# Projections of a 256-token transformer block on plain float32 weights instead of three float32r products

## The reference, cut to what matters

```python
for l in range(2):                                   # first block
    mod = silu(c) @ w_mod[l] + b_mod[l]              # 2048 -> 6144: shift, scale, gate
    h = rmsnorm(x, norm_gain[l]) * (1 + scale) + shift
    proj = h @ w_in[l]                               # 2048 -> 7504 columns
    ...                                              # sparse attention, retention, gates
    x = x + gate * (y @ w_out[l])                    # 2048 -> 2048
# second block, 16 meta tokens ahead of x
proj = rms_norm(h, norm_mix) @ w_in_2                # 2048 -> 7176
...                                                  # stick-breaking and forgetting attention
h = h + merged @ w_out_2                             # 2048 -> 2048
q = rms_norm(h, norm_ffn) @ peer_w_query             # 2048 -> 2048
...                                                  # top 16 of 16384 experts for 8 heads
a = gelu(einsum('thkd,td->thk', u[idx], h))          # 128 rows of 2048 floats for each token
out = h + einsum('thk,thkd->td', g * a, v[idx])
```

## Time and profile before

| | us |
|---|---|
| median of 3 runs | 3126.39 (3125.57 to 3129.42) |
| the profiled execution, its span | 3121.8 |
| TensorE busy | 2089.0 (67%) |
| VectorE busy | 1836.5 (59%) |
| ScalarE busy | 853.8 (27%) |
| GpSimd busy | 800.9 (26%) |
| moved by DMA | 900.9 MB, mean 289 GB/s |

### The profile page before, as it was taken

One profiled execution on the slowest core, in us unless ns is written; L12 is line 12 of the kernel. 1 busy time (PEld: TensorE's weight loads), 2 busy tenths in 40 slices (PEclk: granted clock), 3 DMA queues, 4 the chain that ended last, 5 costly groups with the idle time before them and its releaser, 6 DMA issues.

```text
span 3121.8 us, 29077 instructions
## 1 busy us (share of the span) xinstructions
PE 2089.0 (67%) x11378; PEld 1478.6 (47%) x11378; DVE 1836.5 (59%) x2711; ACT 853.8 (27%) x1267; POOL 800.9 (26%) x680
## 2 busy tenths in 40 slices
PE   5888989989999999999999983223232322322235
PEld 2676777888787787666668871000000000000001
DVE  3679886566776664343336697766565555564430
ACT  1334544444454454544545420000000000000000
POOL 1111110000000000000000036665555555555552
PEclk8999999999999999999999996566656566666667
DMA  9887875557665545334226699999999999999998
GB/s 385 289 293 263 296 259 150 184 182 248 210 189 153 164 158 172 111 122 132 85 82 201 194 377 403 422 422 421 421 422 421 422 421 419 421 421 421 421 421 346
DMA packets 244741, 900.90 MB, mean 289 GB/s; under 512 B 20759, under 2 KB 45613, under 8 KB 178413
## 3 DMA queue, kind: packets, MB, share of 16 engines
q0 software_dynamic: 94208, 612.85, 48.9%
q1 hardware_dynamic: 149152, 284.53, 27.8%
q10 hardware_dynamic: 1244, 1.67, 0.2%
HBM read 894.78 MB, written 2.10 MB: 287 GB/s over the span
## 4 chain that ended last, share of the span: by engine, by line
PE 45%; DMA 29%; DVE 10%; ACT 3%; issue 3%; POOL 2%; ACTq 0%; POOLq 0%; DVEq 0%
PE pp L1818 38%; DMA late<-in_peer_v,MI 9%; DMA P<-in_peer_v,MI 5%; PE tp L1818 5%; DMA x<-in_peer_v,MI 5%; DMA ring<-in_peer_v,MI 4%; DVE wL L1130 3%; DMA SY<-in_peer_v,MI 2%; PE tp L1821 2%; ACT wH L626 1%; DMA ring<-in_peer_w_query 1%; DVE UHM L1286 1%; DMA ring<-in_w_in 1%; POOL late L2361 1%; DVE P L1777 0%
## 5 line engine op out<-in xcount | busy, mean ns | idle before, releaser
L1130 DVE TENSOR_TENSOR wL<-ring,wH 128x1024 fp32r<-128x1024 f32 (+3 forms) x504 | 583.2, 1161 | 573.7 <-ACT wH L626 572.4
L1818 PE MATMUL pp<-wH,hH 128*128 128x512 f32 (+3 forms) x1888 | 745.7, 395 | 35.5 <-DVE wL L1130 19.4
L1818 PE MATMUL pp<-wL,hH 128*128 128x512 f32 (+3 forms) x1888 | 721.4, 382 | 0.0
L1818 PE MATMUL pp<-wH,hL 128*128 128x512 f32 (+3 forms) x1888 | 720.5, 382 | 0.0
L626 ACT ACTIVATE wH<-ring 128x1024 fp32r<-128x1024 f32 (+3 forms) x504 | 508.3, 1011 | 729.7 <-PE pp L1818 548.0
L1818 PE MATMUL pp<-late,S 128*32 128x512 f32 x768 | 232.6, 879 | 335.7 <-DMA x<-in_peer_v,MI 156.3
L1818 PEld LDWEIGHTS pp<-wH,hH 128*128 128x128 f32 x1888 | 362.3, 192 | 141.2 <-issue 46.3
L1818 PEld LDWEIGHTS pp<-wH,hL 128*128 128x128 f32 x1888 | 361.6, 192 | 64.1
L1818 PEld LDWEIGHTS pp<-wL,hH 128*128 128x128 f32 x1888 | 362.8, 192 | 57.3 <-issue 1.0
L1777 DVE CUSTOM_DVE_ANT_0 late<-late,P 128x2048 f32<-128x2048 f32 x84 | 191.2, 2288 | 155.2 <-DMA late<-in_peer_u,MI 155.2
L1818 PE MATMUL pp<-P,S 128*32 128x512 f32 x360 | 162.7, 898 | 166.9 <-DMA late<-in_peer_v,MI 93.2
(11 more groups left out here) (305 smaller groups left out, 2985.2 us busy)
## 6 DMA issues: line engine op xcount, KB each, us to landing
ring<-in_w_in SPq DMA_DIRECT2D x288, 512.0 KB, 4.4
ring<-in_w_out SPq DMA_DIRECT2D x96, 512.0 KB, 4.2
P<-in_w_mod POOLq DMA_DIRECT2D x85, 512.0 KB, 5.1
late<-in_w_mod SPq DMA_DIRECT2D x64, 512.0 KB, 9.4
SY<-in_w_mod POOLq DMA_DIRECT2D x43, 512.0 KB, 5.5
ring<-in_w_in SPq DMA_DIRECT2D x48, 368.0 KB, 4.8
ring<-in_peer_w_query SPq DMA_DIRECT2D x32, 512.0 KB, 7.9
ring<-in_w_in SPq DMA_DIRECT2D x24, 344.0 KB, 3.2
```

Of the source, the lines that this page charges most:

```text
L1130: tt(lo, raw, hi.bitcast(F32), ALU.subtract).then_inc(*tick("dve_lo", *names))
L1818: return e.matmul(o, l, r, start=start, stop=stop, skip_group_check=skip)
```

## The change

Weights and h are no longer cut. `three` becomes one product of plain float32 operands; `wH`, `wL`, `hH`, `hL` and `late` go, one `hT` stays. A piece waits for its load itself and frees the ring slot itself. The ring has 14 slots, and loads are issued 11 pieces ahead. The first 64 loads of w_mod pass through the last 8 ring slots; gathers have 14 buffers, five of them free at once as before, two in `hT` and seven in the ring from the end of p6 on. A chunk of h is written half by ScalarE and half by VectorE, and each half has its own mark. ScalarE has two new waits for its own earlier work ("squared", "attended").

```diff
-NB, NS, NG = 3, 4, 11
+NS, NG = 14, 14
+AHEAD = NS - 3
...
-    def splits(p, q):
-        while asked[0] < min(place[p, q] + NB, len(where)):
-            yield "split", *where[asked[0]]
+    def fetches(p, q):
+        while asked[0] < min(place[p, q] + AHEAD, len(where)):
+            yield "fetch", *where[asked[0]]
             asked[0] += 1
...
-    mod_in = [*[late[:, 1024 * b:1024 * b + 1024] for b in range(8)], P[:, 0, GA:GA + 1024], P[:, 1, GA:GA + 1024],
+    mod_in = [*[ring[:, NS - 8 + b, :] for b in range(8)], P[:, 0, GA:GA + 1024], P[:, 1, GA:GA + 1024],
...
                 if r >= NS:
                     w.wait_ge(*at("ring used", r - NS))
+                elif r >= NS - 8:
+                    w.wait_ge(*at("mod used", 56 + r - (NS - 8)))
...
-                act(heads(wH[k % NB][:, 0:2 * wd], 2), raw, ACT.Copy).then_inc(*tick("act_hi", ("hi", k)))
...
-                tt(lo, raw, hi.bitcast(F32), ALU.subtract).then_inc(*tick("dve_lo", *names))
...
+                    for j in (2, 3):
+                        k = 4 * c + j
+                        ts(hT[:, k, :], tp[u % 2][:, j * 256:j * 256 + 256], mcol[:, l, 16 + k:17 + k], mcol[:, l, k:k + 1],
+                           ALU.mult, ALU.add).then_inc(*tick("dve_h", *([("chunk turned", u), ("chunk", p, c, 1)] if j == 3 else [])))
...
-                w.wait_ge(*at("lo", k))
-                w.wait_ge(*at("chunk", p, pc // 2))
+                raw = heads(ring[:, r % NS, 0:2 * wd], 2)
+                w.wait_ge(*at("raw", r))
+                w.wait_ge(*at("chunk", p, pc // 2, pc % 2))
...
-                        hs = hH[:, kk, t * 128:(t + 1) * 128], hL[:, kk, t * 128:(t + 1) * 128]
-                        m = three(pp[b][:, 0:wd], hs, (hi[:, k2, :], lo[:, k2, :]), kk == 0, kk == 15)
+                        m = mm(pp[b][:, 0:wd], hT[:, kk, t * 128:(t + 1) * 128], raw[:, k2, :], kk == 0, kk == 15)
...
-                elif slot == 5:
-                    w.wait_ge(*at("lo", LAST_CUT))
-                elif slot == 7:
+                elif slot == 5:
                     w.wait_ge(*at("grouped", 6, 3))
```

More of the change, by code:

```diff
@@ L195, in project @@
         for q, (n, c0, w, pc) in enumerate(PIECES[p]):
-            yield from splits(p, q)
+            yield from fetches(p, q)
             if p in (0, 2) and n == 0:
@@ L324, in order @@
     for q, (g, c0, w, pc) in enumerate(PIECES[6]):
-        yield from splits(6, q)
+        yield from fetches(6, q)
         if q == 3:
@@ L404, in mixer_peer_program @@
         rsd = sb("rsd", [128, 6])
[L405 to L410, removed]
+        hT = sb("hT", [128, NK, 256])
         ident = CW[:, ID:ID + 128]
@@ L512, in slots, with parts @@
                 had[i] = n
-        def parts(p, c):
-            step = 2 if p in (1, 3) and c < 2 else 1
-            return [(k, step) for k in range(4 * c, 4 * c + 4, step)]
+        def parts(p, k0):
+            step = 2 if p in (1, 3) and k0 < 8 else 1
+            return [(k, step) for k in range(k0, k0 + 2, step)]
         def gain(p, k):
@@ L582, in sync @@
             for what, *a in order():
-                if what == "split":
+                if what == "fetch":
                     p, q = a
@@ L616, in store_rows @@
                                     xP[q:128:4, t, d * 512:(d + 1) * 512]).then_inc(*landed(sem, ("out", t, d, q)))
[L617 to L625, removed]
-                act(heads(wH[k % NB][:, 0:2 * wd], 2), raw, ACT.Copy).then_inc(*tick("act_hi", ("hi", k)))
+            turn, side = itertools.count(), itertools.count()
             def norm(p):
@@ L823, in sparse @@
                         w.wait_ge(*at("top", l, t, g))
+                        if (t, g) != (0, 0):
+                            w.wait_ge(*at("attended", l, *((t, 0) if g else (t - 1, 1))))
                         for h in range(4):
@@ L1764, in vector @@
                     for b0 in (0, 8):
-                        next(loads)
                         u = next(turn)
@@ L1826, in pair @@
                     w.wait_ge(*at("pair free", had_pair[u % 2]))
+                    if had_pair[u % 2] in by_two:
+                        w.wait_ge(*at("chunk turned", had_pair[u % 2]))
                 had_pair[u % 2] = u
                 return tp[u % 2], u
-            def three(o, l, r, first, final, skip=False):
-                mm(o, l[0], r[0], first, False, skip)
-                mm(o, l[0], r[1], False, False, skip)
-                return mm(o, l[1], r[0], False, final, skip)
             def chunk(p, c):
                 pr, u = pair()
+                by_two.add(u)
                 if p in (1, 3):
@@ L1865, in piece @@
                         kk = pc * 2 + k2
-                        hs = hH[:, kk, t * 128:(t + 1) * 128], hL[:, kk, t * 128:(t + 1) * 128]
-                        m = three(pp[b][:, 0:wd], hs, (hi[:, k2, :], lo[:, k2, :]), kk == 0, kk == 15)
-                    names = [("cut used", k)] if t else []
+                        m = mm(pp[b][:, 0:wd], hT[:, kk, t * 128:(t + 1) * 128], raw[:, k2, :], kk == 0, kk == 15)
+                    names = []
+                    if t and not (p == 4 and meta_part(c0, wd)):
+                        names.append(("ring used", r))
+                    elif t and pc % 2:
+                        names += [("ring used", raw_of[p, q - 1]), ("ring used", r)]
                     if pc == 7:
@@ L2263, in tensor @@
                     tr(pr[:, 512:608], stk2[0:96, :], 96).then_inc(*tick("pe_turned", ("turned", u)))
-                elif what == "split":
+                elif what == "fetch":
                     raw_of[a[0], a[1]] = next(loads)
-                    cut_of[a[0], a[1]] = next(ahead[0])
                 elif what == "chunk":
@@ L2282, in tensor @@
                     n, c0, wd, pc = PIECES[6][a[0]]
-                    k = next(cut)
-                    hi, lo = (heads(b[k % NB][:, 0:2 * wd], 2) for b in (wH, wL))
+                    r = raw_of[6, a[0]]
+                    raw = heads(ring[:, r % NS, 0:2 * wd], 2)
                     if pc == 0:
                         pr6, u6 = pair()
-                    w.wait_ge(*at("lo", k))
-                    w.wait_ge(*at("chunk", 6, pc // 2))
+                    w.wait_ge(*at("raw", r))
+                    w.wait_ge(*at("chunk", 6, pc // 2, pc % 2))
                     for b in range(4):
```

90 lines of the change are left out of this document (32 added, 58 removed).

## The result

| | before | after |
|---|---|---|
| median, 4 runs each (us) | 3126.06 | 3275.42 (3274.48 to 3277.49) |
| ratio, 95% interval | | 1.0481 (1.0462 to 1.0500) |
| span of the profiled execution (us) | 3121.8 | 3272.9 |
| TensorE busy (us) | 2089.0 | 2355.9 |
| VectorE, ScalarE busy (us) | 1836.5, 853.8 | 1253.7, 345.6 |

The change makes the kernel 4.8% slower; 14% faster was forecast. VectorE and ScalarE lost what they were expected to lose, and TensorE gained 267 us where it should have lost some 500.

The account below looks back on a forecast made before the run. PE was taken to bound the projections (DMA in p0 after the change) and DMA the gathers; the stage times summed to 2681 us of span, plus 4.6 gives 2686 us. 2630 to 2780 us held some 82%.

Parts of the forecast that it names:

- What a product costs: Projections p0 to p6: a plain float32 product of 512 columns takes 0.43 us, against 0.6915 for three float32r products.
- Rival (b): Projections: the array passes more often in long accumulating runs, 0.86 to 0.92 us per product, 3410 to 3500 us; chance 3%.
- Rival (a): Projections: a low granted clock makes a plain product 0.86 us or more, kernel ending near 3410 us; chance 3%.
- p0: First projection: bound by DMA at 343 GB/s, 364 us instead of 452.5.
- p1, p3, p5: These projections: TensorE still sets the time, 55, 58.5 and 60.2 us, with loads at 305 GB/s.
- rival (c): Weight loads in p0 to p3 and p5 get 250 GB/s, not 343: + 152, 2838 us; chance 5%.
- p2 and p4: These projections: 290 us (now 405.1) and 395 us (now 504.2), with 8 and 9 us added.
- Rival (d): Chains between pieces bound: PE's 44 us idle in p2 and p4 triples instead of growing by 17, 2756 us; chance 17%.
- p6 to the first gather: Start of p6 up to the first gather of expert rows: 31.5 us, with 9.0 less for products and 1.2 for a split.
- The gathers: First gather to the end: 1313.4 us instead of 1324.4, 11 us less because query weights have landed earlier.
- Start and gap: Start before p0 falls from 104.3 to 101.2 us, gap between p1 and p2 from 13.0 to 9.9.
- The splits: Dropping 504 rounding copies (ScalarE) and 504 subtractions (VectorE): these lie nearly nowhere on PE's path.

Follow-up runs that it names:

- e2: Kernel after, each projection product replaced by two equal bf16 products of the upper halves of the same bytes: 2640.59 us, ratio 0.8441.
- e3: Kernel after, each projection product replaced by a single bf16 product of the upper halves of the same bytes: 2471.54 us, ratio 0.7890.
- e5: Kernel after with the splits put back as unused work TensorE does not wait for, 12 ring slots, 13 gather buffers: 3305.96 us, ratio 1.0565.
- e8: Kernel after with each load waiting for the piece four before it, a ring of 4 in effect: 3309.82 us, ratio 1.0600.
- e9: Kernel before with the plain float32 product in p6 alone and 10 ring slots in p6: 3113.39 us, ratio 0.9970.
- e6: Kernel before with the plain float32 product in p6 alone, ring kept at 4 slots: 3138.64 us, ratio 1.0028.

## Why the prediction was wrong

**The step that failed** is "What a product costs". It read a plain product of 512 columns off as 0.43 us: two instructions, one starting 0.43 us after the other. The distance was right, the kernel after has the same one. The following row is 43 such instructions in a run:

```profile
499.67 18.62 PE L1775 MATMUL pp<-ring,hT 128*128 128x512 f32 x43
```

(18.62 - 0.59) / 42 = 0.429 us. What was wrong is that an instruction of the trace was taken for a product of the program. A product is two of them, 0.86 us. Everything needed was in the kernel before: the order of TensorE's instructions has the index-score step of 128 columns as `x4`, and its trace has the same step as `x8`, like the step of 256 columns in the earlier trace rows:

```profile
214.19 1.05 PE L1818 MATMUL tp<-MI,TAB 128*128 128x128 f32 x8
```

The number was checked for its duration and not for its count. (The `S,CW` products of the earlier trace rows are those of the gate rows and not of bias tables, as the prediction has it; that changes nothing.)

**The rule that was set aside fits the runs.** The Trainium skill, "FP8 and Floating Point Precision", section TensorE Precision Notes, counts four passes for true FP32. The trace agrees in time once the instructions are counted: two of 0.43 us each, and 0.866 us per product in p1 is 3.76 times the 0.2305 of a float32r one, just under the 0.92 that the prediction gave for four. The passes themselves stand in no trace. The prediction said that "the trace has a number for exactly this shape and disagrees"; the trace did not disagree.

**Rival (b)** had the doubling, at 3%, with a wrong reason (that it would need a long accumulating run) and a total too high, 3410 against 3275. Its sum was 1960 us of TensorE work plus 111 us of old idling and gaps between start and end of p6. Measured: 1910 and 14, and the gap of 8.8. Idling of TensorE is filled by longer products; it does not add to them. The granted clock rose to 0.99 to 1.00 in every stage (before 0.95 in p0, 0.96 in p4), and the other work on TensorE got some 40 to 50 us cheaper with it (worked out, not isolated). For the same reason the swap alone cost 221 us and not the some 320 that its terms add up to: 0.866 - 0.6915 = 0.1745 us by 1536 products of 512 columns is 268, the narrower ones and p6 some 55 (estimates); p1 paid its full price (21.7 us for 128 products), p0 37.6 of some 80.

**Rival (a)**, a low clock, is excluded: TensorE at 1.00 in p1 to p6.

**Point by point, the rest of the sum.** With products at 0.45 us (e2) it came out 45 us under the forecast, 2641 against 2686.
- *p0*: 482.7 to p1's first group against 479, bound by DMA in the main, but at 320 GB/s over the stretch instead of 343 and with waits for VectorE that the sum had not: that the two numbers lie so near is in part luck.
- *p1, p3, p5*: 3.5 to 7 us over the forecast for three groups each, of which 0.02 us by 96 products is 2 and the way the marks are set 1. The loads reach nearly what they need, and 370 GB/s around p1 of e3 excludes the 250 of rival (c).
- *p2 and p4*: 13 and 34 us under. The idling did not grow, and p4's nearly vanished. Rival (d) had the sign wrong: without splits in the queues the chains between pieces run faster, and e5 gives part of the reason (the rest is argued).
- *p6 to the first gather*: 30.7 against 31.5.
- *The gathers*: 1301.5 against 1313.4, so 23 us are won (17 in the kernel after) where 11 were forecast. The forecast put them in the right place, but laid them to query weights landed earlier, which is at most a small part: between the first and the 22nd gather the deep ring is worth 4 us (e8) or nothing (e9 against e6). The runs show two things that the prediction did not see: 14 to 17 us because dot products no longer stand behind splits (e6, and after against before), and a deep ring that spares a stall of some 30 us at the 23rd gather (e8, e6 and e9).
- *Start and gap*: 3.1 us forecast for each; 4.7 and 4.2 measured.
- *The tail* at 421 GB/s stayed as it was: 1248.2 us before, 1248.6 after.
- *The splits*: "On PE's path they lie nearly nowhere, as PE is full in p1, p3, p5" holds there: e5 agrees to the tenth of a us. Over the rest of the kernel they cost some 30 us even where TensorE does not wait for them (e5).

So the account from before to after is: + 221 for the product, - 31 for the splits' time in the queues (e5, with its smaller ring), and - 40 that is left over, laid to TensorE's waits on splits, chunks and the shallow ring and not isolated; together + 150 (measured 149).

## What to carry to other kernels

Before a row of the trace is used as the price of an operation, count its instructions against the calls in the program; a price per instruction times the number of calls is off by whatever the ratio is. Where a rule on the chip and a row seem to disagree by a round factor, look for that factor in the counting first. Work added to the busiest engine first fills its idle time, and work taken off the others can be worth more than their waits show, through whatever stands behind it in their queues.

## What the runs showed of the hardware

- A plain float32 product is carried out as two instructions, each starting 0.43 us after the last at 512 columns and 0.216 at 256 columns: 0.866 us per product of 512 columns in a full stage. A float32r product is one instruction and takes 0.2305. Three of these are cheaper (0.69) than one plain product.
- A bf16 product that reads every second 16-bit element of float32 data, stationary and moving, starts every 0.226 us at 512 columns (e2), about as a float32r one does.
- Kept full, TensorE held a granted clock of 0.99 to 1.00 for 1900 us; from 2100 to 3000 us, among the gathers, it stands at 0.63 in both kernels, with TensorE busy for 29% of the time.
- Weight loads moved at 370 GB/s at a DMA share of 1.01 (around p1 of e3), while gathers of whole 8 KB expert rows hold 421.
